# Gate and up columns taken 512 at a time instead of 256 in the dense layer and the experts

## The chip, the cores and the metric

One core of one Trainium2 chip. The metric is the device time of one execution in microseconds. The kernel before took 1407.61 us (median of 3 runs, 1405.66 to 1407.75).

## The reference, cut to what matters

Two layers on 256 tokens of width 1024. Each layer mixes the tokens (four mixers of 256 columns each) and then runs a feed-forward part: the first a dense SwiGLU, the second eight experts with two experts per token. D_FF is 2816. All in float32.

```
def swiglu(t, w_gate, w_up, w_down):
    return (jax.nn.silu(t @ w_gate) * (t @ w_up)) @ w_down
u = rms_norm(h, norm2_g[l])
f = swiglu(u, ffn_w_gate[j], ffn_w_up[j], ffn_w_down[j])          # layer 0
f = moe_ffn(u, moe_router[j], moe_w_gate[j], moe_w_up[j], moe_w_down[j])   # layer 1: swiglu of each routed token
h = h + f
```

## The kernel before, in words

**Weights stream through a ring.** All large weights are cut into pieces of 128 partitions x 2048 floats (1 MB). SyncE (SP) loads them in order into a ring of 11 slots, two DMAs a piece (L366). For each piece ScalarE (ACT) writes a rounded copy `high` (`split_high`, L531) and VectorE (DVE) the rest, `low` = piece - high (`split_low`, L861). Both have 3 slots, so the high of piece n waits until TensorE (PE) has used piece n-3 (`piece_used`). SP may load piece n when the low of piece n-11 is done. Every product is three matmuls: high x high, high x low, low x high (L1528 to L1530, L1504 to L1506).

**The feed-forward function `ffn`** stands once on each of ACT (L582), DVE (L900) and PE (L1488). It is called for the dense layer with two tiles of 128 tokens and for each expert job with one tile. It walks over 11 chunks of 256 gate and 256 up columns. The pieces of chunk c are a and b (four and four of the eight 128-row blocks, each row block with 256 gate and 256 up columns side by side, so one matmul of 512 columns gives both, in bank[t]) and d (256 rows of the down matrix). The order is a(0) b(0) a(1) b(1) d(0) a(2) b(2) d(1) ... b(10) d(9) d(10): 33 pieces (L61). With one tile a piece is 12 matmuls of 512 columns.

For chunk c the engines do:

- PE: the products of a and b; the down product of chunk c-1; then, when DVE's `hid` is there, two transposes for each tile into bank 4 (L1541). Chunk 10 is followed by its own down product (L1543).
- ACT: silu of the gate half (`sg`, L600), then the highs of the next pieces, then the rounded copy of the transposed block (`hTh`, L607).
- DVE: up x silu (`hid`, L916, L918 in the dense layer), lows, then `hTl` = bank 4 - hTh (L925).

**An expert job** works on the tokens of one expert; eight jobs run here, and none of the three spare ones. The work between jobs hangs on fixed chunks of the running job j: the result of job j-1 is rounded (`result_high` L825, `result_low` L1371) after the high and low of piece 1, and scattered by PE in chunk 0 (L1834); DVE adds it to h (`add_result`, L1379) in chunks 0 and 1; `slots` (L838, L1844) runs in chunk 2; DVE's selection of the next tokens in chunk 4 (L1394); PE gathers them in chunk 6 (L1816), ACT and DVE copy them out (`tokens_out`, L813, L1359), and PE transposes them in chunk 8 (L1825). At the last chunk ACT and DVE split these tokens (`tokens_high` L818, `tokens_low` L1364). In the first job DVE also plans the spare jobs in chunk 1 (`route_overflow`, L1320).

Of the kernel before, what the change touches and what calls it, by code (L numbers as in the profile page):

```python
# [56 lines left out]
CHUNKS = 11  # L57
N_FFN = 3 * CHUNKS
# [12 lines left out]

FFN_ORDER = ffn_pieces()
FFN_AT = {key: n for n, key in enumerate(FFN_ORDER)}

# [17 lines left out]
def build(nc, x, positions, norm1_g, w_in, mlstm_conv_w, mlstm_conv_b, mlstm_gate_b,  # L92
# [14 lines left out]
    F_CH = moe_w_gate.shape[3] // CHUNKS  # L107
    assert (TT, KD, F_CH, E) == (2, 8, 256, 8)
# [10 lines left out]
    with ctx:  # L119
# [102 lines left out]
        with ExitStack() as part:  # L222
            sg = sb("sg", [P, TT, 256], F32, part)
            hid = sb("hid", [P, TT, 256], F32, part)
            hTh = sb("hTh", [P, 2, TT, P], F32R, part)
            hTl = sb("hTl", [P, 2, TT, P], F32R, part)
# [74 lines left out]
        SLOTS_AT, SELECT_AT, GATHER_AT = 2, 4, 6  # L301
# [63 lines left out]
        def _(sp):  # L365
# [33 lines left out]
            def load_ffn(n0, wg, wu, wd, rounds=None):  # L399
                for i, (kind, c) in enumerate(FFN_ORDER):  # L400
                    n = n0 + i
                    if kind == "d":
                        dst = slot(n).rearrange("p (f n) -> p f n", f=2)
                        src = wd.rearrange("(f p) n -> p f n", p=P)
                        load(n, [(dst[:, f:f + 1, :], src[:, 2 * c + f:2 * c + f + 1, :]) for f in (0, 1)], rounds)
                    else:
# [3 lines left out]
                                  w.rearrange("(k p) n -> p k n", p=P)[:, k0:k0 + 4, c * F_CH:(c + 1) * F_CH])  # L410
# [117 lines left out]
        def _(act):  # L528
# [53 lines left out]
            def ffn(n0, job, job_n, tiles, after_split={}, after_chunk={}, after_last=None, scale=None, start=0):  # L582

# [10 lines left out]
                for c in range(CHUNKS):  # L594
                    at = FFN_AT[("b", c)]
# [22 lines left out]
            for l in range(DEPTH):  # L618
# [165 lines left out]
                if l == 0:  # L784
# [6 lines left out]
                    ffn(DENSE0, None, 0, TT, scale=rstd, start=2)  # L791
# [40 lines left out]
            def job(j, first):  # L832
# [8 lines left out]
                def next_tokens():  # L841

                    act.wait_ge(s["piece_used"], N_FFN * j + (MOE0 + FFN_AT[("b", CHUNKS - 1)] + 1))
# [14 lines left out]
        def _(dve):  # L858
# [41 lines left out]
            def ffn(n0, job, job_n, tiles, after_split={}, after_chunk={}, after_last=None, scale=None, start=0):  # L900
# [8 lines left out]
                for c in range(CHUNKS):  # L909
                    at = FFN_AT[("b", c)]  # L910
# [3 lines left out]
                    for t in range(tiles):  # L914
                        if scale is None:
                            last = dve.tensor_tensor(hid[:, t, :], bank[t][:, 256:512], sg[:, t, :], ALU.mult)  # L916
                        else:
                            last = dve.scalar_tensor_tensor(out=hid[:, t, :], in0=bank[t][:, 256:512], scalar=scale[:, t, 0:1],  # L918
                                                            in1=sg[:, t, :], op0=ALU.mult, op1=ALU.mult)
# [4 lines left out]
                    dve.wait_ge(s["hTh_ready"], job_n * CHUNKS + (c + 1))  # L924
                    dve.tensor_tensor(hTl[:, :, 0:tiles, :],  # L925
                                      bank[4][:, 0:2 * tiles * P].rearrange("p (f t n) -> p f t n", f=2, t=tiles),
                                      hTh[:, :, 0:tiles, :].bitcast(F32), ALU.subtract).then_inc(s["hTl_ready"], 1)
# [45 lines left out]
            for l in range(DEPTH):  # L973
# [271 lines left out]
                if l == 0:  # L1245
# [3 lines left out]
                    ffn(DENSE0, None, 0, TT, scale=rstd, start=2)  # L1249
# [129 lines left out]
            def add_result(n, t):  # L1379

                for half in range(2):
                    i = 2 * t + half
                    dve.wait_ge(s["scat_ready"], 4 * n - (3 - i))
                    dst = h[:, t, half * 512:(half + 1) * 512]
                    last = dve.tensor_tensor(dst, bank[SCATTER_BANKS[i]][:, :], dst, ALU.add).then_inc(s["added"], 1)

            def job(j, first):
# [16 lines left out]
                def chunk1():  # L1404
                    if first:
                        route_overflow()
                    else:
                        add_result(j, 1)
# [11 lines left out]
            for t in range(TT):  # L1420
                add_result(n_jobs, t)
# [12 lines left out]
        def _(pe):  # L1434
# [53 lines left out]
            def ffn(n0, job, job_n, tiles, xT, accs, first_claims, after_products={}):  # L1488


# [3 lines left out]
                def down(c):  # L1494
                    n = n0 + FFN_AT[("d", c)]
                    pe.wait_ge(s["hTl_ready"], at(c + 1))
                    pe.wait_ge(s["low_ready"], pieces + (n + 1))
                    for f in range(2):
# [391 lines left out]
```

## Time and profile before

| | |
|---|---|
| median of 3 runs | 1407.61 us |
| the profiled execution: device time / span | 1403.45 / 1401.7 us |
| PE busy | 1308.3 us (93%) |
| DVE busy | 1040.5 us (74%) |
| ACT busy | 825.3 us (59%) |
| read from HBM | 345.68 MB |
| dense `ffn` (first product to last) | 185.95 to 378.6 us |
| expert jobs (first product to last) | 570.97 to 1386.3 us |

The times of the table and of the rows come from one profiled execution. PE, DVE and ACT run beside each other, so their busy times don't add up. A matmul of 512 columns stands in the trace with some 390 ns, but the next one starts about 0.23 us after it: matmuls overlap, and the start-to-start distance is what counts.

### The profile page before, as it was taken

The numbers are of one execution on the slowest core, as the hardware profiler recorded it, in microseconds if no ns is written. First come the engines' busy times: TensorE is split into PE (matmuls) and PEld (weight loads), VectorE is DVE, ScalarE is ACT, GpSimd is POOL, SyncE is SP. The second block draws the span as 40 slices with busy tenths as digits, with TensorE's granted clock in tenths as the row PEclk, the third lists the DMA queues.
The fourth block names the chain that finished last, engine by engine and source line by source line (L and its number), as shares of the span: only waits on it lengthen the run. The fifth ranks groups of instructions, "written<-read, shape, count | busy, mean of one in ns | idle before, by whom it ended". The sixth has DMA issues, their size and how long they took to land.

```text
span 1401.7 us, 18029 instructions
## 1 busy us (share of the span) xinstructions
PE 1308.3 (93%) x6301; PEld 1081.8 (77%) x6301; DVE 1040.5 (74%) x1117; ACT 825.3 (59%) x886; POOL 33.3 (2%) x77
## 2 busy tenths in 40 slices
PE   4989979999899897899999999999999999999996
PEld 4967868888699586678788788787787887887884
DVE  4873645445469465588888988888988988988985
ACT  5333643344434264457776777777777677776774
POOL 4001000000000000000000000000000000000000
PEclk9986899999989868799999999999999999999998
DMA  9920345556354014489999999999999999999961
GB/s 303 321 79 2 113 155 189 181 183 176 115 188 151 1 60 136 148 294 345 333 352 350 321 362 346 325 365 342 317 354 331 350 347 333 342 353 338 344 225 46
DMA packets 267217, 347.43 MB, mean 248 GB/s; under 512 B 13166, under 2 KB 238592, under 8 KB 267168
## 3 DMA queue, kind: packets, MB, share of 16 engines
q1 hardware_dynamic: 265904, 344.43, 72.8%
q0 software_dynamic: 1232, 2.33, 0.7%
q8 instruction: 31, 0.51, 0.1%
q14 instruction: 18, 0.15, 0.0%
q10 hardware_dynamic: 32, 0.01, 0.0%
HBM read 345.68 MB, written 1.05 MB: 247 GB/s over the span
## 4 chain that ended last, share of the span: by engine, by line
PE 84%; DVE 11%; ACT 3%; issue 1%; DMA 1%; SPq 0%; DVEq 0%; ACTq 0%
PE bank L1528 15%; PE bank L1530 14%; PE bank L1529 14%; PE bank L1504 7%; PE bank L1505 7%; PE bank L1506 7%; DVE low L865 4%; DVE cacc L1005 3%; ACT high L538 2%; PE bank L1541 2%; PE bank L1816 1%; PE bank L1477 1%; PE bank L1478 1%; PE bank L1479 1%; PE bank L1772 1%
## 5 line engine op out<-in xcount | busy, mean ns | idle before, releaser
L865 DVE TENSOR_TENSOR low<-ring,high 128x2048 fp32r<-128x2048 f32 x327 | 743.0, 2283 | 166.7 <-ACT high L538 165.9
L538 ACT ACTIVATE high<-ring 128x2048 fp32r<-128x2048 f32 x327 | 623.1, 1908 | 168.6 <-PE bank L1530 99.6
L1528 PE MATMUL bank<-high,uTh 128*128 128x512 f32 x880 | 354.5, 403 | 11.8 <-DVE low L865 5.2
L1530 PE MATMUL bank<-high,uTl 128*128 128x512 f32 x880 | 346.1, 393 | 0.0
L1529 PE MATMUL bank<-low,uTh 128*128 128x512 f32 x880 | 344.7, 392 | 0.0
L1528 PEld LDWEIGHTS bank<-high,uTh 128*128 128x128 f32 x880 | 166.6, 189 | 46.8 <-DVE low L865 8.2
L1530 PEld LDWEIGHTS bank<-high,uTl 128*128 128x128 f32 x880 | 166.4, 189 | 36.3
L1529 PEld LDWEIGHTS bank<-low,uTh 128*128 128x128 f32 x880 | 166.9, 190 | 32.3
L1504 PE MATMUL bank<-high,hTh 128*128 128x512 f32 x440 | 176.8, 402 | 12.7 <-DVE hTl L925 9.4
L1505 PE MATMUL bank<-low,hTh 128*128 128x512 f32 x440 | 174.7, 397 | 0.0
L1506 PE MATMUL bank<-high,hTl 128*128 128x512 f32 x440 | 174.4, 396 | 0.0
L607 ACT ACTIVATE hTh<-bank 128x256 fp32r<-128x256 f32 (+1 forms) x99 | 40.2, 407 | 141.9 <-PE bank L1541 141.9
L1504 PEld LDWEIGHTS bank<-high,hTh 128*128 128x128 f32 x440 | 83.2, 189 | 35.6 <-issue 12.4
L1506 PEld LDWEIGHTS bank<-high,hTl 128*128 128x128 f32 x440 | 83.6, 190 | 19.9
L1505 PEld LDWEIGHTS bank<-low,hTh 128*128 128x128 f32 x440 | 83.6, 190 | 18.6
L600 ACT ACTIVATE sg<-bank 128x256 f32<-128x256 f32 x88 | 33.9, 386 | 70.4 <-PE bank L1530 70.4
L925 DVE TENSOR_TENSOR hTl<-bank,hTh 128x256 fp32r<-128x256 f32 (+1 forms) x99 | 44.5, 449 | 31.7 <-ACT hTh L607 31.7
L1477 PE MATMUL bank<-high,uTh 128*128 128x256 f32 (+2 forms) x192 | 54.1, 282 | 0.0
L1478 PE MATMUL bank<-low,uTh 128*128 128x256 f32 (+2 forms) x192 | 53.8, 280 | 0.0
L1479 PE MATMUL bank<-high,uTl 128*128 128x256 f32 (+2 forms) x192 | 53.7, 280 | 0.0
L1477 PE MATMUL bank<-uTh,high 128*128 128x256 f32 x160 | 47.3, 296 | 6.1 <-DVE uTl L895 6.1
L1005 DVE SCALAR_TENSOR_TENSOR cacc<-glu,cols,cacc 128x256 f32<-128x256 f32 x120 | 52.6, 508 | 0.0
(373 smaller groups left out, 1319.2 us busy)
## 6 DMA issues: line engine op xcount, KB each, us to landing
ring<-in_moe_w_gate_dram SPq DMA_DIRECT2D x176, 512.0 KB, 4.9
ring<-in_moe_w_up_dram SPq DMA_DIRECT2D x176, 512.0 KB, 6.1
ring<-in_moe_w_down_dram SPq DMA_DIRECT2D x176, 512.0 KB, 5.5
ring<-in_w_in_dram SPq DMA_DIRECT2D x36, 512.0 KB, 5.9
ring<-in_ffn_w_gate_dram SPq DMA_DIRECT2D x22, 512.0 KB, 4.0
ring<-in_ffn_w_up_dram SPq DMA_DIRECT2D x22, 512.0 KB, 5.0
ring<-in_ffn_w_down_dram SPq DMA_DIRECT2D x22, 512.0 KB, 3.8
ring<-in_w_out_dram SPq DMA_DIRECT2D x16, 512.0 KB, 6.2
```

What stands on the lines that cost most here:

```text
L538: act.activation(high[:, n % SPLIT, 0:width], slot(n)[:, 0:width], ACT.Copy).then_inc(s["high_ready"], 1)
L865: dve.tensor_tensor(low[:, n % SPLIT, 0:width], slot(n)[:, 0:width], high[:, n % SPLIT, 0:width].bitcast(F32), ALU.subtract).then_inc(s["l ...
L1005: ins = dve.scalar_tensor_tensor(out=cacc[:, c, :], in0=taps, scalar=w, in1=cacc[:, c, :], op0=ALU.mult, op1=ALU.add)
L1477: pe.matmul(dst, ah, bh, start=first, stop=False)
L1478: pe.matmul(dst, ah, bl, start=False, stop=False)
L1479: last = pe.matmul(dst, al, bh, start=False, stop=final)
L1504: pe.matmul(o, ah, bh, start=(c == 0 and f == 0), stop=False)
L1505: pe.matmul(o, ah, bl, start=False, stop=False)
L1506: last = pe.matmul(o, al, bh, start=False, stop=(c == CHUNKS - 1 and f == 1))
L1528: pe.matmul(o, ah, bh, start=(kd == 0), stop=False)
L1529: pe.matmul(o, ah, bl, start=False, stop=False)
L1530: last = pe.matmul(o, al, bh, start=False, stop=(kd == KD - 1))
```

## The change

Five chunks of 512 gate and 512 up columns and one of 256, in place of eleven of 256. A wide chunk has pieces u0, u1 (up, row blocks 0 to 3 and 4 to 7), g0, g1 (gate) and two down pieces d0, d1; the last chunk has a, b and d0 as before. The order is u0 u1 g0 g1 (0), then for c = 1 to 4 u0 u1 g0 g1 (c) d0 d1 (c-1), then a b (5) d0 d1 (4) d0 (5): still 33 pieces of 1 MB and two DMAs each. A gate or up row of a wide chunk is 2 KB in memory; it was 1 KB. Up goes to bank 0 (bank 1 for the second tile), gate to bank 4 (7 for the second), and the transposes of hid go over the gate bank. ACT, DVE and PE take a wide chunk with one instruction of 512 columns where there were two chunks with one of 256 each.

The order of the pieces and the chunks at which the work between jobs hangs:

```diff
 def ffn_pieces():
     for c in range(CHUNKS):
-        order += [("a", c), ("b", c)]
+        order += [("u0", c), ("u1", c), ("g0", c), ("g1", c)] if c < LAST else [("a", c), ("b", c)]
         if c:
-            order.append(("d", c - 1))
-    return order + [("d", CHUNKS - 1)]
+            order += [("d0", c - 1), ("d1", c - 1)]
+    return order + [("d0", LAST)]
...
-        SLOTS_AT, SELECT_AT, GATHER_AT = 2, 4, 6
+        UP_BANKS, GATE_BANKS = (0, 1), (4, 7)
+        DENSE_ACC, MOE_ACC = ((2, 3), (5, 6)), ((2, 3),)
+        SLOTS_AT, GATHER_AT = 2, 3
```

`ffn` on ACT (`product_end(c)` is the index of g1, or of b in the last chunk; `blocks(c)` is 4, in the last chunk 2):

```diff
                 for c in range(CHUNKS):
-                    at = FFN_AT[("b", c)]
+                    at = product_end(c)
+                    w = 128 * blocks(c)
                     upto(at + 2)
...
-                        last = act.activation(sg[:, t, :], bank[t][:, 0:256], ACT.Silu,
+                        gate = bank[GATE_BANKS[t] if c < LAST else UP_BANKS[t]]
+                        last = act.activation(sg[:, t, 0:w], gate[:, 0:w], ACT.Silu,
                                               scale=1.0 if scale is None else scale[:, t, 0:1])
                     last.then_inc(s["silu_ready"], 1)
-                    if c == CHUNKS - 1 and after_last:
+                    upto(at + (3 if c in (0, LAST) else 4))
+                    if c == LAST and after_last:
                         after_last()
-                    upto(at + 3)
                     act.wait_ge(s["hid_tr"], job_n * CHUNKS + (c + 1))
-                    act.activation(hTh[:, :, 0:tiles, :],
-                                   bank[4][:, 0:2 * tiles * P].rearrange("p (f t n) -> p f t n", f=2, t=tiles),
-                                   ACT.Copy).then_inc(s["hTh_ready"], 1)
+                    for t in range(tiles):
+                        last = act.activation(hTh[:, 0:blocks(c), t, :],
+                                              bank[GATE_BANKS[t]][:, 0:w].rearrange("p (f n) -> p f n", n=P), ACT.Copy)
+                    last.then_inc(s["hTh_ready"], 1)
...
-                ffn(MOE0, j, j + 1, 1, {} if first else {1: lambda: result_high(j)},
+                ffn(MOE0, j, j + 1, 1, MOE_TILES, {} if first else {2: lambda: result_high(j)},
```

`ffn` on DVE and what a job hangs into it:

```diff
                     last.then_inc(s["hid_ready"], 1)
-                    if c == CHUNKS - 1 and after_last:
+                    after_hid.get(c, lambda: None)()
+                    upto(at + (3 if c in (0, LAST) else 4))
+                    dve.wait_ge(s["hTh_ready"], job_n * CHUNKS + (c + 1))
...
+                    last.then_inc(s["hTl_ready"], 1)
+                    if c == LAST and after_last:
                         after_last()
-                    upto(at + 3)
...
-                ffn(MOE0, j, j + 1, 1, {} if first else {1: lambda: result_low(j)},
-                    {0: chunk0, 1: chunk1, SELECT_AT: next_select, GATHER_AT: lambda: tokens_out(j + 1)},
+                        add_result(j, 2)
+
+                ffn(MOE0, j, j + 1, 1, MOE_TILES, {} if first else {2: lambda: result_low(j)},
+                    {} if first else {1: lambda: add_result(j, 1), 2: lambda: add_result(j, 3)},
+                    {0: chunk0, 1: chunk1, SLOTS_AT: next_select, GATHER_AT: lambda: tokens_out(j + 1)},
```

`ffn` on PE (a product piece is 12 matmuls for each tile, as before, into one bank):

```diff
+                def hidden_transposes(c):
+                    pe.wait_ge(s["hid_ready"], at(c + 1))
+                    for t in range(tiles):
+                        for f in range(blocks(c)):
+                            last = pe.transpose(bank[GATE_BANKS[t]][:, f * P:(f + 1) * P], hid[:, t, f * P:(f + 1) * P], ident[:, :])
+                    last.then_inc(s["hid_tr"], 1)
...
                 for c in range(CHUNKS):
+                    if c < LAST:
+                        products("u0", c)
+                        products("u1", c)
+                        if c:
+
+                            pe.wait_ge(s["hTl_ready"], at(c))
+                        products("g0", c)
+                        products("g1", c)
+                    else:
+                        products("a", c)
+                        products("b", c)
                     if c:
...
+                        down(c - 1, 0)
+                        if c < LAST:
+                            down(c - 1, 1)
                     after_products.get(c, lambda: None)()
...
+                    hidden_transposes(c)
+                down(LAST - 1, 1)
+                down(LAST, 0)
...
-                        GATHER_AT + 2: lambda: gathered_transposes(j + 1)}
+                        GATHER_AT + 1: lambda: gathered_transposes(j + 1)}
```

In the expert jobs `add_result` now adds one quarter at a time: quarters 0 and 2 after hTl of chunks 0 and 1, quarters 1 and 3 after hid of chunks 1 and 2. `route_overflow` stays in chunk 1.

## Rows read from the trace of the kernel before

**Rows 1.** The page, part 4: the chain that ended last, by engine.
```profile
PE 84%; DVE 11%; ACT 3%; issue 1%; DMA 1%; SPq 0%; DVEq 0%; ACTq 0%
```

**Rows 2.** Windows, one expert job: length, engines' busy us (instructions), PEclk, DMA share, GB/s.
```profile
840.40:941.40 101.00, 99.21 (x450) 80.69 (x449) 88.42 (x69) 72.27 (x62) 0.00 (x0) 1.00 1.00 343
```

**Rows 3.** Waits of PE and of SP's DMA queue in the same job: us, times, longest.
```profile
PE bank L1504 <- DVE hTl L925: 1.0, 1, 1.0
PE bank L1528 <- DVE low L865: 0.8, 1, 0.8
...
SPq L375 <- DVE low L865: 62.9, 33, 5.1
```

**Rows 4.** Timeline of PE at a job's end: start us, us, instruction, idle before.
```profile
877.00 0.38 PE L1541 MATMUL bank<-ident,hid 128*128 128x128 f32 x2
878.39 0.49 PE L1504 MATMUL bank<-high,hTh 128*128 128x512 f32 x1 [1.01 <-DVE hTl L925]
...
881.04 0.39 PE L1506 MATMUL bank<-high,hTl 128*128 128x512 f32 x1
882.21 0.50 PE L1528 MATMUL bank<-high,uTh 128*128 128x512 f32 x1 [0.78 <-DVE low L865]
```

**Rows 5.** Timeline of PE where nothing is waited for: transposes, two pieces, down.
```profile
951.69 0.38 PE L1541 MATMUL bank<-ident,hid 128*128 128x128 f32 x2
951.83 0.47 PE L1528 MATMUL bank<-high,uTh 128*128 128x512 f32 x1
952.14 0.39 PE L1529 MATMUL bank<-low,uTh 128*128 128x512 f32 x1
...
957.40 0.40 PE L1504 MATMUL bank<-high,hTh 128*128 128x512 f32 x1
```

**Rows 6.** Timeline of ACT at a job's end and the next one's start.
```profile
877.42 0.38 ACT L607 ACTIVATE hTh<-bank 128x256 fp32r<-128x256 f32 x1 [1.66 <-PE bank L1541]
877.91 3.72 ACT L538 ACTIVATE high<-ring 128x2048 fp32r<-128x2048 f32 x2
881.54 1.25 ACT L829 ACTIVATE yh<-bank,wslot 128x512 fp32r<-128x512 f32 x2
```

**Rows 7.** Timeline of DVE at the same place.
```profile
876.17 1.28 DVE L1367 TENSOR_TENSOR uTl<-bank,uTh 128x512 fp32r<-128x512 f32 x2
...
879.86 4.49 DVE L865 TENSOR_TENSOR low<-ring,high 128x2048 fp32r<-128x2048 f32 x2 [1.60 <-ACT high L538]
884.27 1.40 DVE L1375 SCALAR_TENSOR_TENSOR yl<-bank,wslot,yh 128x512 fp32r<-128x512 f32 x2
```

**Rows 8.** Groups by line and shape: count, busy us, mean ns, idle before.
```profile
L916 DVE TENSOR_TENSOR hid<-bank,sg 128x256 f32<-128x256 f32 x88 | 36.8, 418 | 13.0 <-ACT sg L600 13.0
...
L925 DVE TENSOR_TENSOR hTl<-bank,hTh 128x512 fp32r<-128x512 f32 x11 | 7.6, 691 | 20.0 <-ACT hTh L607 20.0
L607 ACT ACTIVATE hTh<-bank 128x512 fp32r<-128x512 f32 x11 | 6.6, 597 | 35.5 <-PE bank L1541 35.5
```

**Rows 9.** Dense layer: PE's waits in the layer, then ACT and DVE in chunk 0.
```profile
PE bank L1541 <- DVE hid L918: 1.8, 1, 1.8
PE bank L1504 <- DVE hTl L925: 1.4, 1, 1.4
...
199.62 0.84 ACT L600 ACTIVATE sg<-bank,rstd 128x256 f32<-128x256 f32 x2 [3.46 <-PE bank L1530]
200.49 0.88 DVE L918 SCALAR_TENSOR_TENSOR hid<-bank,rstd,sg 128x256 f32<-128x256 f32 x2 [6.33 <-ACT sg L600]
```

**Rows 10.** First job's long wait (timeline of PE); windows after it and at the kernel's end.
```profile
598.14 0.76 PE L1504 MATMUL bank<-high,hTh 128*128 128x512 f32 x1 [3.33 <-DVE low L865]
...
598.10:603.40 5.30, 5.26 (x12) 4.02 (x13) 4.63 (x3) 0.00 (x0) 0.00 (x0) 0.50 0.78 252
...
1386.30:1389.30 3.00, 0.15 (x1) 0.00 (x0) 1.41 (x2) 2.55 (x3) 0.00 (x0) 1.00 0.02 5
1389.30:1393.00 3.70, 3.51 (x8) 2.26 (x8) 1.65 (x4) 0.72 (x1) 0.00 (x0) 0.54 0.00 0
```

More of the change, by code:

```diff
@@ L222, in build @@
         with ExitStack() as part:
[L223 to L226, printed above, removed]
+            sg = sb("sg", [P, TT, WIDE], F32, part)
+            hid = sb("hid", [P, TT, WIDE], F32, part)
+            hTh = sb("hTh", [P, 4, TT, P], F32R, part)
+            hTl = sb("hTl", [P, 4, TT, P], F32R, part)
+        with ExitStack() as part:
+            moe_sg = sb("moe_sg", [P, 1, WIDE], F32, part)
+            moe_hid = sb("moe_hid", [P, 1, WIDE], F32, part)
+            moe_hTh = sb("moe_hTh", [P, 4, 1, P], F32R, part)
+            moe_hTl = sb("moe_hTl", [P, 4, 1, P], F32R, part)
             unh = sb("unh", [P, TT, D], F32R, part)
@@ L298, in build @@
         SCATTER_BANKS = (1, 5, 6, 7)
-        SLOTS_AT, SELECT_AT, GATHER_AT = 2, 4, 6
+        UP_BANKS, GATE_BANKS = (0, 1), (4, 7)
+        DENSE_ACC, MOE_ACC = ((2, 3), (5, 6)), ((2, 3),)
+        DENSE_TILES, MOE_TILES = (sg, hid, hTh, hTl), (moe_sg, moe_hid, moe_hTh, moe_hTl)
+        SLOTS_AT, GATHER_AT = 2, 3
         fin_g = ring[:, 0, 0:D]
@@ L580, in group_rstd, with ffn @@
                 act.activation(rstd[:, :, g:g + 1], lnv[:, :, g:g + 1], ACT.Exp, scale=-0.5).then_inc(s["group_rstd"], 1)
-            def ffn(n0, job, job_n, tiles, after_split={}, after_chunk={}, after_last=None, scale=None, start=0):
+            def ffn(n0, job, job_n, tiles, sets, after_split={}, after_chunk={}, after_last=None, scale=None, start=0):
+                sg, _, hTh, _ = sets
                 done = [start]
@@ L898, in gains_of, with ffn @@
                 last.then_inc(s["utl_ready"], 1)
-            def ffn(n0, job, job_n, tiles, after_split={}, after_chunk={}, after_last=None, scale=None, start=0):
+            def ffn(n0, job, job_n, tiles, sets, after_split={}, after_hid={}, after_chunk={}, after_last=None, scale=None, start=0):
+                sg, hid, hTh, hTl = sets
                 done = [start]
@@ L1377, in result_low, with add_result @@
                 last.then_inc(s["yl_ready"], 1)
[L1379 to L1385, printed above, removed]
+            def add_result(n, i):
+                t, half = divmod(i, 2)
+                dve.wait_ge(s["scat_ready"], 4 * n - (3 - i))
+                dst = h[:, t, half * 512:(half + 1) * 512]
+                dve.tensor_tensor(dst, bank[SCATTER_BANKS[i]][:, :], dst, ALU.add).then_inc(s["added"], 1)
             def job(j, first):
@@ L1486, in uT, with ffn, products, down @@
                 return uTh[:, k, lo:hi], uTl[:, k, lo:hi]
-            def ffn(n0, job, job_n, tiles, xT, accs, first_claims, after_products={}):
+            def ffn(n0, job, job_n, tiles, sets, xT, accs, first_claims, after_products={}):
+                _, hid, hTh, hTl = sets
                 pieces = N_FFN * job if job is not None else 0
                 at = lambda c: job_n * CHUNKS + c
-                def down(c):
-                    n = n0 + FFN_AT[("d", c)]
+                def products(kind, c):
+                    n = n0 + FFN_AT[(kind, c)]
+                    kh = {"u0": 0, "g0": 0, "a": 0, "u1": 1, "g1": 1, "b": 1}[kind]
+                    pe.wait_ge(s["low_ready"], pieces + (n + 1))
+                    if job is None and c == 0 and kind[0] == "u":
+                        pe.wait_ge(s["utl_ready"], 4 * 2 + 2 * (kh + 1))
+                    for t in range(tiles):
+                        o = bank[GATE_BANKS[t] if kind[0] == "g" else UP_BANKS[t]][:, :]
+                        for k in range(4):
+                            kd = 4 * kh + k
+                            ah, al = xT(kd, t)
+                            bh, bl = part(n, k * 512, (k + 1) * 512)
+                            pe.matmul(o, ah, bh, start=(kd == 0), stop=False)
+                            pe.matmul(o, ah, bl, start=False, stop=False)
+                            last = pe.matmul(o, al, bh, start=False, stop=(kd == KD - 1))
+                    last.then_inc(s["piece_used"], 1)
+                def down(c, half_of):
+                    n = n0 + FFN_AT[(f"d{half_of}", c)]
                     pe.wait_ge(s["hTl_ready"], at(c + 1))
                     pe.wait_ge(s["low_ready"], pieces + (n + 1))
-                    for f in range(2):
+                    for i in range(2):
+                        f = 2 * half_of + i
                         for t in range(tiles):
@@ L1502, in down @@
                                 ah, al = hTh[:, f, t, :], hTl[:, f, t, :]
[L1503 removed]
+                                bh, bl = part(n, i * 1024 + half * 512, i * 1024 + half * 512 + 512)
                                 pe.matmul(o, ah, bh, start=(c == 0 and f == 0), stop=False)
                                 pe.matmul(o, ah, bl, start=False, stop=False)
[L1506 removed]
+                                last = pe.matmul(o, al, bh, start=False, stop=(c == LAST and f == 1))
```

92 lines of the change are left out of this document (38 added, 54 removed).

## Prediction, made before the change was run

> **What bounds the kernel now.** I read the chain of waits first: PE holds 84% of it, DVE 11% [rows 1]. The longest stage is the eight expert jobs, so I looked at one job by windows: 101.0 us, of which PE is busy 99.2, DVE 88.4 and ACT 72.3, with the granted clock at 1.00, the upper of its two levels (2.4 GHz) [rows 2]. The waits of that job say what PE lacks: it waits only twice, once at its end for hTl (1.0 us) and once at the next job's first product for a low (0.8 us) [rows 3]. Everything else is matmuls end to end. The arithmetic of a job is the same after the change (88 products and 44 down products, each of three matmuls of 512 columns, and 22 transposes), so its floor is the same too. What can change is these two waits, new waits of the same kind, and the clock.
>
> **Durations.** Two product pieces (24 matmuls) take 5.57 us (951.83 to 957.40), a piece 2.8 us; two transposes take 0.14 us to the next product, whose first step is 0.31 instead of 0.23 us [rows 5]. Four transposes I put at 0.36. PE waiting costs, beyond the wait, about 0.1 us of slower first step (the same row; after transposes it is paid anyway).
>
> **Part 1: the last chunk's wait goes.** Before, the transposes of chunk 10 start at 877.00 and the down product that needs them at 878.39, 1.39 us, against 0.14 where nothing is waited for [rows 4, 5]; nothing is left for PE to do meanwhile. After, d1(4), 2.8 us, stands between the transposes of the last chunk and d0(5). Is hTl there in time? Count from the start of d0(4). ACT: silu 0.2 to 0.6; high of the last piece (two take 3.72 [rows 6], so 1.9) to 2.4; tokens_high, as long as DVE's 1.28 pair at most [rows 7], to 3.6; hTh to 4.0. DVE: low of the last piece (2.2 to 2.3 [rows 7]) to 4.7, hTl 0.4, to 5.1. PE wants it at 2.8 + 0.14 + 2.8 = 5.7. So 1.25 us a job are saved, 8 x 1.25 = **-10.0 us**.
>
> **Part 2: the wait at a job's start nearly goes.** Before, the last down matmul starts at 881.04 and the next job's first at 882.21: 1.17 where 0.23 is normal, 0.94 lost and 0.1 of restart [rows 4]; the high of piece 0 begins behind hTh at 877.91 and the low at 879.86 [rows 6, 7]. Seven times: -7.2. After, going on with the count: DVE does tokens_low behind hTl, 5.1 + 1.3 = 6.4, then the low of the next job's piece 0 to 8.6 or 8.7, and ACT's high of it is done by 5.9. PE is at the next job at 2.8 + 0.14 + 2.8 + 2.8 = 8.55. I take 0.1 us of wait and 0.1 of restart, +1.4 in seven jobs. Net **-5.8 us**. Pieces 1 to 3 follow at a low every 2.2 us against 2.8 on PE; result_low (1.40 [rows 7]) stands ahead of piece 3's low, which ends some 7.9 us after the job's start, and PE wants it at 8.2.
>
> **Part 3: a new chain, in each wide chunk.** g0(c+1) overwrites the gate bank with the transposes in it, and its high is made behind hTh. PE covers this with u0 and u1, 5.57 us. The chain, from the start of u0: hTh starts at 0.28 (877.42 is 0.42 after 877.00 [rows 4, 6], less the 0.14 to the next product), takes 0.60 [rows 8], high 1.9, low 2.3, and 0.1 to PE: 5.2. It holds by 0.4 us where nothing is hung in between. In chunk 2, selT and wslot stand between hTh and high; I put them at 0.4, so it is even. In chunk 3, tokens_out, a copy as wide as hTh (0.60 [rows 8]), makes it 5.8: 0.2 of wait and 0.1 of restart, 8 x 0.3 = **+2.4 us**. Bounds: nothing (if the copies overlap by 0.1 each, as the pairs do: 1.25 for two), or 0.5 in both chunks, +8. hTl itself (0.69 [rows 8]) is ready about 1.6 after u0 starts if DVE is free, at the worst behind a low and an addition, 3.5, still in time.
>
> **Part 4: instructions saved.** Two of 256 columns become one of 512: hid 2 x 0.418 to 0.69, and so hTl (0.69), sg and hTh (0.60 against 2 x 0.38) [rows 8, 6]. DVE gains about 1.5 us a job and ACT as much. Neither ends a wait by its sum, so in the total this is 0; it helps DVE, which is at 88 of 101 us, to keep parts 2 and 3 in time.
>
> **Part 5: the dense layer.** Its last-chunk wait of 1.4 us [rows 9] goes under d1(4), twice as long here (two tiles): **-1.5 us** with the restart. In chunk 0 nothing covers silu and hid: before, PE waits 1.8 us for a pair of each, 0.84 and 0.88 [rows 9]. 512 wide, a pair with a scale takes 1.25 on ACT and 1.40 on DVE [rows 6, 7]: 0.41 + 0.52 = **+0.9 us**, and the wait becomes 2.8.
>
> **Part 6: the clock after that wait.** In this trace a wait of 1.8 us left the clock at its upper level. After 3.33 us of idle PE it stood at 0.50, 1.2 GHz, and 12 matmuls took 5.3 us where 2.8 is normal; after the 2.9 us of idle at the kernel's end it stood at 0.54 [rows 10]. 2.8 is nearest to that last one, so I take a fall of the clock once, **+2.5 us**; the bounds are 0 and 3. The waits of up to 1.4 us elsewhere don't come near.
>
> **Part 7: the first expert job.** In chunk 0 there is no scatter to cover silu and hid: 0.60 and 0.69 in place of 0.38 and 0.42, **+0.5 us** [rows 6, 8]. In the other jobs the scatter, eight matmuls or 1.8 us, covers the 1.6 they need. Its 3.3 us wait behind route_overflow [rows 10] stays: those small instructions again stand between an hTl and the low that PE wants next as before, and u0, u1 cover as much as a, b did. 0, bounds -1 and +1.
>
> **Part 8: transfers.** In a job SP's queue waits 62.9 of 101 us for a free slot [rows 3], and no high waits for a transfer, so faster transfers give 0. The same 34.6 MB in 99.2 us need 349 GB/s in place of 343 [rows 2].
> The Trainium skill, "DMA: Bandwidth & Descriptors", section "Why small descriptors are slow (HBM only)", charges each packet three fixed cycles beside one for each 32 bytes. By an estimate from that page 2 KB rows spend 4.5% on them and 1 KB rows 8.6%, so that a stage bound by transfers would gain some 3%, and one bound by PE nothing. No row here shows 2 KB rows.
>
> **Sum.** -10.0 - 5.8 + 2.4 - 1.5 + 0.9 + 2.5 + 0.5 = -11.0 us. The profiled execution took 1403.45 us, so it would take 1392.5; the median of the runs is 4.2 us higher than the profiled one, and against it the forecast is 1407.6 - 11.0 = **1396.6 us**. 0.2% of it, 2.8 us, is about what a measurement can tell from no change.
>
> **Rivals.**
> (A) All chains of parts 2, 3 and 6 end in time: no +1.4, +2.4, +2.5; -17.3, 1390.3 us. For it speak the overlaps of about 0.1 us between neighbours on one engine, against it the idle row at the end. Chance 0.10.
> (B) The waits removed come back in part: parts 2 and 3 at their upper bounds, a start wait of 0.5 us (+2.8 more) and +8 in place of +2.4: 1405 would be the worst, the middle 1401. DVE's order (low, hTl, tokens_low, low) has no slack at the job's start, which speaks for it. Chance 0.12.
> (C) Slower: in every wide chunk the chain of part 3 is late. Four places a job are followed by a g0, 32 in all. The forecast's -11 is used up at 0.34 us a place with the restart, that is if the chain lasts 0.64 us longer than my 5.2. If DVE is 1 us behind there, because lows, additions and hTl queue up (88 of 101 us busy), PE waits 0.6 + 0.1: 32 x 0.7 = 22, less the 2.4 counted: 1416 us. Against it: the chunks without extras leave DVE idle before each low, as they do now. Chance 0.07.
> (D) The clock doesn't hold. PE now writes its products by turns to two banks and the down products to two more. If it fell once a job at the price of rows 10, 2.5 us, the time would be 1396.6 + 20 = 1417 us. The granted clock of 1.00 through a job that already changes banks every 12 or 24 matmuls and waits 1 us twice [rows 2, 3] speaks against it. Chance 0.03.
> The Trainium skill, "TensorE: Matmul & The Clock Gate", section "A second HAM failure mode: psum-queue depth-cycling", reports for another kernel that cycling through banks idles PE so often that its clock goes up and down; by that rule (D) would come. The trace of before doesn't agree, at 1.00.
> (E) The change doesn't do what it says for the experts, because 343 GB/s is all the transfers give: DMA share 1.00 [rows 2]. Then a job stays at 101 us and only the dense layer and the clock count, -1.5 + 0.9 + 2.5 + 0.5 = +2.4: 1410 us. SP's queue waiting 62.9 us for slots speaks against it. Chance 0.05.
>
> **Chances and range.** The forecast has 0.63. Faster by over 0.2% are the forecast, (A) and most of (B): 0.84; within 0.2%: a rest of (B) and a part of (E), 0.05; slower: (C), (D), most of (E): 0.11. The range from 1390 to 1403 us holds the forecast with its bounds, (A) and most of (B), and leaves out some 0.18.
>
> **What the changed profile would show.** A job of 99.1 us by windows; no wait of L1504's successor for hTl in the last chunk; the first product of a job 0 to 0.3 us after its time; at most 0.3 us before g0 in chunk 4; in the dense layer one wait of 2.8 us before the first transposes, and the clock after it at 0.5. Wrong would be: a wait before g0 in chunks 1 and 2 (then part 3's chain is mis-sized, C), a job that still takes 101 us with highs waiting for a DMA (E), or a granted clock under 1.00 within the jobs (D).

## The result and the profile after

Median of four runs after: 1387.82 us (1382.03 to 1390.85); of four before: 1406.63 us (1403.36 to 1407.75). The ratio is 0.9865, with a 95% interval of 0.9828 to 0.9902. So the change saves 18.8 us where 11.0 were forecast. The sign was right; the time lies 2.2 us under the range, and the forecast's own gain is outside the interval. The profiled execution took 1387.18 us, its span is 1385.3 us, against 1403.45 and 1401.7.

First the page of after, parts 1, 2 and 4 (busy us and share of the span, DMA packets, the chain that ended last). The last answers to [rows 1]:

```profile
PE 1308.3 (94%) x6301; PEld 1089.4 (79%) x6301; DVE 1032.4 (75%) x1028; ACT 817.7 (59%) x797; POOL 32.9 (2%) x77
...
DMA packets 175057, 347.43 MB, mean 251 GB/s; under 512 B 13166, under 2 KB 54272, under 8 KB 175008
...
PE 87%; DVE 10%; ACT 1%; issue 1%; DMA 1%; SPq 0%; DVEq 0%; ACTq 0%
```

PE's share of the chain rose from 84 to 87%, DVE's fell from 11 to 10. Packets fell from 267,217 to 175,057. Where the time went stands in the windows. Here those of before, from the first product to the last down product of the dense layer, of the mixers between, and of the eight expert jobs (length, busy us and instructions of PE, PEld, DVE, ACT, POOL, granted clock, DMA share, GB/s):

```profile
185.95:378.58 192.63, 189.38 (x836) 154.80 (x836) 89.81 (x65) 81.68 (x74) 0.00 (x0) 0.99 0.54 172
378.60:571.00 192.40, 163.92 (x970) 143.35 (x969) 127.61 (x251) 83.69 (x158) 9.64 (x13) 0.80 0.31 105
570.97:1386.30 815.33, 797.82 (x3576) 648.25 (x3576) 701.14 (x561) 571.33 (x491) 0.00 (x0) 0.99 0.95 322
```

And after, with one steady job, which answers to [rows 2]:

```profile
187.56:379.25 191.69, 188.89 (x836) 154.96 (x836) 87.59 (x56) 80.26 (x65) 0.00 (x0) 0.99 0.54 173
379.30:576.50 197.20, 170.79 (x969) 149.41 (x969) 127.71 (x251) 83.81 (x158) 9.67 (x13) 0.78 0.30 102
576.53:1370.48 793.95, 789.35 (x3576) 647.24 (x3576) 694.77 (x481) 564.92 (x411) 0.00 (x0) 1.00 0.93 331
...
843.65:942.15 98.50, 98.50 (x450) 80.91 (x449) 87.61 (x59) 71.48 (x52) 0.00 (x0) 1.00 0.98 352
```

By the starts of their first and last matmuls the dense layer went from 192.4 to 191.5 us (-0.9), the experts from 815.1 to 793.7 (-21.4). The mixers between them went from 192.6 to 197.5 (+4.9) although nothing in them was changed: the same 970 matmuls were busy for 170.8 in place of 163.9 us at a granted clock of 0.78 in place of 0.80. The start of the kernel is 1.6 us longer and the tail 0.5 shorter. Together -16.3 us, the difference of the two profiled executions; that of the medians is 2.5 more (one of the four runs on either side was profiled). The two changed stages alone differ by -22.3.

In the steady job PE is busy for all of 98.50 us, and no matmul of it waits. The queue of SP still waits for slots, for 61.6 of 98.5 us, as in [rows 3]:

```profile
SPq L397 <- DVE low L895: 61.6, 33, 4.8
```

At the job's end, PE and then DVE (start, us, instruction, idle before), for [rows 4, 7]:

```profile
872.14 0.38 PE L1570 MATMUL bank<-ident,moe_hid 128*128 128x128 f32 x2
872.28 0.48 PE L1561 MATMUL bank<-high,moe_hTh 128*128 128x512 f32 x1
...
877.71 0.40 PE L1563 MATMUL bank<-high,moe_hTl 128*128 128x512 f32 x1
877.95 0.39 PE L1544 MATMUL bank<-high,uTh 128*128 128x512 f32 x1
```

```profile
873.97 0.42 DVE L958 TENSOR_TENSOR moe_hTl<-bank,moe_hTh 128x256 fp32r<-128x256 f32 x1
874.31 1.28 DVE L1403 TENSOR_TENSOR uTl<-bank,uTh 128x512 fp32r<-128x512 f32 x2
875.50 6.89 DVE L895 TENSOR_TENSOR low<-ring,high 128x2048 fp32r<-128x2048 f32 x3
```

Both waits are gone. The last down matmul starts at 877.71 and the next job's first product at 877.95, 0.24 us, the normal step; before it was 1.17 [rows 4]. The low that it needs starts at 875.50 and takes 2.3 of the 6.89 us, so it ends at 877.8, just ahead.

The dense layer's first chunk and the first job's long wait (PE), for [rows 9, 10]:

```profile
214.87 1.09 PE L1570 MATMUL bank<-ident,hid 128*128 128x128 f32 x8 [2.80 <-DVE hid L951]
...
617.87 0.47 PE L1544 MATMUL bank<-high,uTh 128*128 128x512 f32 x1 [3.18 <-DVE low L895]
```

```profile
214.80:220.00 5.20, 5.13 (x27) 4.41 (x28) 5.20 (x5) 1.46 (x3) 0.00 (x0) 1.00 0.34 91
617.80:623.00 5.20, 5.13 (x23) 4.30 (x24) 4.44 (x3) 1.92 (x1) 0.00 (x0) 1.00 0.77 260
```

The dense wait is 2.80 us, as worked out, but the clock behind it stands at 1.00. It also stands at 1.00 behind the 3.18 us of the first job, where it fell to 0.50 before [rows 10].

In what follows a gap is the time from one matmul's start to the next one's; where it should be 0.23 us, what is above that is the wait. It holds a little more than the idle time in brackets, since a matmul's end reaches past its successor's start.

### The profile page after: what moved, and what is told of

It reads as the page before. It is cut to its first block, busy times and chain, and to the rows that moved or that the text cites. A ratio compares the mean times of both kernels' runs of the same rounds, so it can differ in the third digit from the quotient of the medians.

```text
span 1385.3 us, 17674 instructions
## 1 busy us (share of the span) xinstructions
PE 1308.3 (94%) x6301; PEld 1089.4 (79%) x6301; DVE 1032.4 (75%) x1028; ACT 817.7 (59%) x797; POOL 32.9 (2%) x77
## 2 busy tenths in 40 slices
DMA packets 175057, 347.43 MB, mean 251 GB/s; under 512 B 13166, under 2 KB 54272, under 8 KB 175008
## 4 chain that ended last, share of the span: by engine, by line
PE 87%; DVE 10%; ACT 1%; issue 1%; DMA 1%; SPq 0%; DVEq 0%; ACTq 0%
PE bank L1544 15%; PE bank L1546 14%; PE bank L1545 14%; PE bank L1561 7%; PE bank L1562 7%; PE bank L1563 7%; DVE cacc L1041 3%; DVE low L895 2%; PE bank L1570 2%; PE bank L1867 1%; PE bank L1514 1%; PE bank L1515 1%; PE bank L1516 1%; PE bank L1823 1%; PE bank L1824 1%; PE bank L1825 1%
## 5 line engine op out<-in xcount | busy, mean ns | idle before, releaser
L1544 PE MATMUL bank<-high,uTh 128*128 128x512 f32 x880 | 350.0, 398 | 9.9 <-DVE uTl L925 4.0
L1561 PE MATMUL bank<-high,moe_hTh 128*128 128x512 f32 x352 | 139.9, 397 | 0.0
L1562 PE MATMUL bank<-low,moe_hTh 128*128 128x512 f32 x352 | 138.9, 395 | 0.0
L1563 PE MATMUL bank<-high,moe_hTl 128*128 128x512 f32 x352 | 138.9, 394 | 0.0
L1563 PEld LDWEIGHTS bank<-high,moe_hTl 128*128 128x128 f32 x352 | 66.3, 188 | 15.7
L1562 PEld LDWEIGHTS bank<-low,moe_hTh 128*128 128x128 f32 x352 | 66.5, 189 | 15.1
L1561 PEld LDWEIGHTS bank<-high,moe_hTh 128*128 128x128 f32 x352 | 66.3, 188 | 14.9
L637 ACT ACTIVATE moe_hTh<-bank 128x512 fp32r<-128x512 f32 (+1 forms) x48 | 27.1, 564 | 68.3 <-PE bank L1570 68.3
L629 ACT ACTIVATE moe_sg<-bank 128x512 f32<-128x512 f32 (+1 forms) x48 | 27.1, 564 | 38.5 <-PE bank L1546 38.5
L1515 PE MATMUL bank<-uTl,high 128*128 128x256 f32 x160 | 47.2, 295 | 0.0
```

Of the source, the lines that this page charges most:

```text
L1515: pe.matmul(dst, ah, bl, start=False, stop=False)
L1544: pe.matmul(o, ah, bh, start=(kd == 0), stop=False)
L1561: pe.matmul(o, ah, bh, start=(c == 0 and f == 0), stop=False)
L1562: pe.matmul(o, ah, bl, start=False, stop=False)
L1563: last = pe.matmul(o, al, bh, start=False, stop=(c == LAST and f == 1))
```

## The experiments

Each ratio is against runs of the kernel before on the same chip: 1409.08 us in experiments 1 to 4 (14 runs), 1408.04 in 5 to 8 (11 runs), 1411.98 in 9 (3 runs).

**1. The tail order alone, on the kernel before.** The last chunk of a job has its second down half behind the transposes and its hidden blocks in the unused second tile slot:

```diff
                     if c:
-                        down(c - 1)
+                        down(c - 1, (0,) if tail else (0, 1))
...
                     last.then_inc(s["hid_tr"], 1)
+                    if tail:
+                        down(c - 1, (1,))
```

> The kernel before, still with chunks of 256 and 1 KB rows, but in the last chunk of an expert job the transposes stand in the middle of d(9), so that six matmuls (1.4 us) lie between them and the last down product. Theory 1 (the gain of the expert jobs is the two waits at a job's end and start, and the order there removes both; width and rows give nothing): a job falls from 101.0 to 98.7 to 99.2 us, the whole by 14 to 18 us. Theory 2 (wider instructions and 2 KB rows give it): a job stays at 100.7 to 101.0 us. In between, about 99.8: only the end wait goes and the start wait stays.

1402.48 us, ratio 0.9955 (0.994 to 0.997); a job takes 100.38 us. PE at the job's end:

```profile
878.81 0.44 PE L1546 MATMUL bank<-ident,hid 128*128 128x128 f32 x2 [0.55 <-DVE hid L917]
879.00 0.48 PE L1507 MATMUL bank<-high,hTh 128*128 128x512 f32 x1
...
884.08 0.50 PE L1532 MATMUL bank<-high,uTh 128*128 128x512 f32 x1 [0.60 <-DVE low L866]
```

None of the three expectations held: the order alone gives 0.6 of the 2.5 us a job. The wait for hTl is gone, but a wait of 0.55 us for hid stands in front of the transposes, and of the 0.78 at the next job's start 0.60 stay. In the kernel before one down piece, 12 matmuls or 2.8 us, stands between the last two chunks, and cut in two it leaves 1.4 us on either side of the transposes. That is enough for hTh and hTl, but silu and hid take 0.7 us longer than that (the gap there is 0.94 in place of 0.23), and the next job's first high still begins behind hTh. With wide chunks the narrow last one follows a chunk with two down pieces, so that a whole piece, 2.8 us, stands on either side, and a piece more, 5.6 us in place of 4.2, between the transposes and the next job, for the low that starts it. So what counts is the order together with the wide chunk ahead of it.

One thing beside the point turns up here: behind the dense layer's first wait, 1.84 us of idle as in the kernel before and with the same code up to there, the clock fell.

```profile
202.00:206.00 4.00, 4.00 (x14) 3.25 (x13) 4.00 (x3) 0.98 (x2) 0.00 (x0) 0.61 0.24 48
```

**2. The tail order undone, on the kernel after.** Both down pieces of chunk 4 stand again ahead of the last transposes:

```diff
-                        if c < LAST:
-                            down(c - 1, 1)
+                        down(c - 1, 1)
...
-                down(LAST - 1, 1)
                 down(LAST, 0)
```

> The changed kernel with both down pieces of chunk 4 ahead of the last transposes, so that nothing stands between these and the last down product. Theory 1: the end wait of about 1.25 us comes back in every job, and the start wait in part, as the high of the next job's first piece is again behind a late hTh: a job of 99.8 to 100.9 us in place of 98.5. Theory 2: a job stays at 98.5 to 98.7 us.

1402.4 us over ten runs, 1390.31 to 1410.66, ratio 0.9952 (0.9915 to 0.999). The scatter is wide, the profile is plain: a steady job takes 100.77 us. PE at its end:

```profile
875.43 0.49 PE L1561 MATMUL bank<-high,moe_hTh 128*128 128x512 f32 x1 [1.01 <-DVE moe_hTl L958]
...
879.24 0.50 PE L1544 MATMUL bank<-high,uTh 128*128 128x512 f32 x1 [0.78 <-DVE low L895]
```

These are the two waits of before to the hundredth, 1.01 and 0.78 us [rows 4]. 2.3 of the 2.5 us a job hang on this order of PE in the last chunk, given the wide chunk ahead of it (experiment 1); parts 1 and 2 are shown. The kernel after also has another order on ACT (the last high ahead of tokens_high) and on DVE (hTl ahead of tokens_low) there. It stands in this run too, so by itself it ends neither wait; whether the gain needs it, no run tests. The mixers took 191.8 us here at a clock of 0.81 with the code of after, so their 197.5 us isn't forced by the change.

**3. The rows alone undone, on the kernel after.** The same 2048 columns of a piece in two transfers of 256 columns of every row:

```diff
-load(n, [(dst[:, k:k + 2, :], src[:, k0 + k:k0 + k + 2, c * WIDE:(c + 1) * WIDE]) for k in (0, 2)], rounds)
+load(n, [(dst[:, :, g:g + 256], src[:, k0:k0 + 4, c * WIDE + g:c * WIDE + g + 256]) for g in (0, 256)], rounds)
```

> The changed kernel with 1 KB rows: each wide piece is loaded in two DMAs of 256 columns. Theory 1 (PE bounds the jobs, transfers have slack): a job stays at 98.5 us and the whole within 0.2%. Theory 2 (2 KB rows are needed for 98.5 us): a job of 99.5 to 101 us, with highs waiting for a DMA.

1389.83 us, ratio 0.9863 (0.9843 to 0.9882), that of after being 0.9865. The steady jobs start 98.47 to 98.51 us apart, in after 98.50 to 98.53. One of them by windows, and SP's queue in it:

```profile
837.30:935.80 98.50, 98.50 (x450) 80.92 (x449) 87.64 (x59) 71.48 (x52) 0.00 (x0) 1.00 1.03 349
...
SPq L397 <- DVE low L895: 59.0, 33, 4.4
```

The queue waits 59.0 us for slots in place of 61.6, and 267,217 packets carry what 175,057 did. What the rows do change is the transfer engines' busy share: 1.03 at 349 GB/s with 1 KB, 0.98 at 352 with 2 KB in the job above, some 5% less time for a byte. In the time of the kernel the 2 KB rows are worth nothing here.

**4. One more copy in the chain ahead of g0.** Behind hTh in chunks 0 to 3 of each job, on the kernel after:

```diff
                     last.then_inc(s["hTh_ready"], 1)
+                    if job is not None and c < LAST - 1:
+                        act.activation(sg[:, 0, :], sg[:, 0, :], ACT.Copy)
```

> The changed kernel with one more ACT copy of 512 columns (about 0.5 us) between hTh and the next high, in chunks 0 to 3 of each job; it measures the slack of the chain hTh, high, low, g0. If neighbours on an engine overlap by 0.1 us (chain 5.0 us plain, 5.3 in chunk 2, 5.5 in chunk 3, against 5.57 of cover): waits of 0.2 to 0.3 us in chunk 2 and 0.4 to 0.5 in chunk 3, none in chunks 0 and 1, a job of 99.0 to 99.5 us. If the prediction's sum of full durations were right (5.2, 5.6, 5.8): waits in chunks 1, 2 and 3 of 0.2, 0.6 and 0.8, a job of about 100.3 us.

1396.58 us, ratio 0.9916 (0.9894 to 0.9938). A job took 99.70 us, +1.2, 0.2 above what was expected for the shorter chain and 0.6 under that for the longer. 0.9 of it are two gaps: 0.59 us behind chunk 2 (0.36 of wait) and 0.76 behind chunk 3 (0.53). Some 0.1 of slower restart each comes with chunks 1 and 2, where the gap behind chunk 1 is 0.26; chunk 0 took the copy without a trace. The last product ahead of chunk 3's gap and the one behind it, then ACT there:

```profile
853.81 0.39 PE L1548 MATMUL bank<-high,uTl 128*128 128x512 f32 x1
854.57 0.50 PE L1546 MATMUL bank<-high,uTh 128*128 128x512 f32 x1 [0.37 <-DVE low L897]
```

```profile
848.78 0.60 ACT L637 ACTIVATE moe_hTh<-bank 128x512 fp32r<-128x512 f32 x1 [3.14 <-PE bank L1572]
849.27 0.62 ACT L641 ACTIVATE moe_sg<-moe_sg 128x512 f32<-128x512 f32 x1
849.79 0.59 ACT L848 ACTIVATE u<-bank 128x512 f32<-128x512 f32 x1
850.27 1.92 ACT L566 ACTIVATE high<-ring 128x2048 fp32r<-128x2048 f32 x1
```

Starts are 0.49, 0.52 and 0.48 us apart where the rows say 0.60, 0.62 and 0.59: neighbours on an engine overlap by about 0.1 us. So the copy costs 0.52 in the chain, and all of it (0.53) shows as a wait in chunk 3. In other words chunk 3 had hardly any slack and no wait, chunk 2 had 0.16 and chunk 1 about 0.5. The same place in the kernel after, PE, ACT and DVE:

```profile
944.34 0.48 PE L1544 MATMUL bank<-high,uTh 128*128 128x512 f32 x1
...
949.89 0.50 PE L1544 MATMUL bank<-high,uTh 128*128 128x512 f32 x1
...
944.62 0.60 ACT L637 ACTIVATE moe_hTh<-bank 128x512 fp32r<-128x512 f32 x1 [3.15 <-PE bank L1570]
945.11 0.59 ACT L846 ACTIVATE u<-bank 128x512 f32<-128x512 f32 x1
945.59 3.72 ACT L566 ACTIVATE high<-ring 128x2048 fp32r<-128x2048 f32 x2
...
947.54 4.49 DVE L895 TENSOR_TENSOR low<-ring,high 128x2048 fp32r<-128x2048 f32 x2 [1.00 <-ACT high L566]
```

From 944.34 to the end of the first low at 949.83 (a pair of them takes 4.49, one 2.29) are 5.49 us, and u0 and u1 last 5.55.

**5. One more operation behind tokens_low, on DVE, in the last chunk:**

```diff
                     if c == LAST and after_last:
                         after_last()
+                        dve.tensor_tensor(hid[:, 0, :], sg[:, 0, :], sg[:, 0, :], ALU.mult)
```

> The changed kernel with one more DVE operation of 512 columns (about 0.5 to 0.6 us) behind tokens_low; it measures the slack of the chain at a job's start (hTl, tokens_low, low of piece 0, first product). The trace of the changed kernel shows 0.1 us of slack there: a wait of 0.3 to 0.5 us at seven job starts with 0.1 of restart, a job of 98.9 to 99.1 us. By the prediction's part 2, which had no slack, 0.1 more. If the start hung on ACT's high instead, a job stays at 98.5 us.

1390.97 us, ratio 0.9882 (0.9847 to 0.9917); a job took 99.07 us. DVE and PE at the job's start:

```profile
877.75 0.68 DVE L964 TENSOR_TENSOR moe_hid<-moe_sg 128x512 f32<-128x512 f32 x1
878.35 4.49 DVE L895 TENSOR_TENSOR low<-ring,high 128x2048 fp32r<-128x2048 f32 x2
...
880.69 0.50 PE L1545 MATMUL bank<-high,uTh 128*128 128x512 f32 x1 [0.33 <-DVE low L895]
```

The extra operation moves the low by 0.60 us and the gap is 0.73, a wait of 0.50. So the slack at the job's start was 0.1 us, where part 2 had put a wait of 0.1.

**6. The overflow work of the first job spread out.** What route_overflow did at once behind chunk 1 is done behind chunks 0, 1, 2 and 4, on the kernel after:

```diff
-                    if first:
-                        route_overflow()
+                    if first:
+                        overflow_job(0)
...
+                def chunk2():
+                    next_select()
+                    if first:
+                        overflow_job(1)
+
+                def chunk4():
+                    overflow_job(2)
+                    overflow_end()
```

> The changed kernel with route_overflow in parts, one for each spare job, behind hTl of chunks 0, 1, 2 and 4 of the first job. The wait of 3.3 us before g0 of chunk 2 goes, and no fall of the clock can follow it: the experts' stage falls from 793.7 to about 790.3 us, the periods of the other jobs stay at 98.5 us. Against the kernel before a ratio of 0.984. Rival: the wait is only cut into pieces before several g0, 1 us or more of it left.

1381.35 us, ratio 0.9816 (0.9786 to 0.9847). The experts take 790.4 us, 3.3 less than after. PE's waits in the first 65 us of the expert stage, in full:

```profile
PE bank L1561 <- DVE uTl L1409: 2.7, 1, 2.7
PE bank L1587 <- DVE moe_hid L949: 1.4, 1, 1.4
```

The 3.18 us wait is gone, nothing takes its place.

**7. The gate products ahead of the up products in chunk 0,** so that silu is made under the up products, on the kernel after:

```diff
+        if c == 0:
+            order += [("g0", c), ("g1", c), ("u0", c), ("u1", c)]
...
-                    act.wait_ge(s["piece_used"], (N_FFN * job if job is not None else 0) + (n0 + at + 1))
+                    act.wait_ge(s["piece_used"], (N_FFN * job if job is not None else 0) + (n0 + (at + 1 if c else 2)))
...
+                    if c == 0:
+                        dve.wait_ge(s["piece_used"], (N_FFN * job if job is not None else 0) + (n0 + at + 1))
```

> The changed kernel with gate ahead of up in chunk 0, so that silu runs under the up products and only hid is left behind them. Dense layer: the wait before the first transposes falls from 2.96 to about 1.65 us; first job: from 1.57 to about 0.95 us; the later jobs, where the scatter covers it, stay at 98.5 us. Sum -1.9 us. Rival: the highs of pieces 4 and 5, which now come behind silu, are late and a wait of the same size stands before u0 or u1 of chunk 1.

1385.81 us, ratio 0.9848 (0.982 to 0.9876). The first transposes of the dense layer, the first job's long wait and a window behind it:

```profile
209.49 1.09 PE L1575 MATMUL bank<-ident,hid 128*128 128x128 f32 x8 [1.57 <-DVE hid L956]
...
607.05 0.47 PE L1549 MATMUL bank<-high,uTh 128*128 128x512 f32 x1 [3.18 <-DVE low L898]
...
607.00:612.30 5.30, 5.25 (x16) 4.22 (x17) 4.30 (x2) 0.77 (x1) 0.00 (x0) 0.68 0.76 267
```

The dense layer took 190.0 us, 1.5 less (its gap went from 3.19 to 1.96), and the first job's gap before its transposes from 1.80 to 1.24. The experts as a whole stayed at 793.8, because here the clock fell for 3.4 us after the first job's long wait, which is the same in code and length as in after. That costs more than the 0.56 of the gap; against it the clock stood at its lower level for 3.7 us at the start of the stage and not 5.4.

**8. Both, 6 and 7 together.**

> Both edits of the two runs before in the changed kernel: -5.2 us against it if they add up, about 1382.5 us and a ratio to the kernel before of 0.983; the experts' stage 789.7 us and the dense layer 190.2 us. If the mixers' clock differs as between the profiles so far (their stage took 191.8 to 197.5 us), the single profile can hide it; the two stages can't.

1382.49 us, ratio 0.9808 (0.9776 to 0.984). Its windows for the dense layer and the experts:

```profile
185.90:376.30 190.40, 188.83 (x836) 155.03 (x836) 87.67 (x56) 80.34 (x65) 0.00 (x0) 0.99 0.52 174
...
575.30:1365.50 790.20, 789.29 (x3576) 647.08 (x3576) 695.46 (x481) 565.82 (x411) 0.00 (x0) 1.00 0.93 333
```

The dense layer is 1.2 us under after and the experts 3.7. In the totals experiments 6 and 8 can't be told apart: the runs of either spread by 6 to 12 us, and the mixers took 199.1 us in the profile of 8 and 197.6 in that of 6. Both are faster than the kernel before; that they are faster than the change alone is shown by the stages, while the intervals of the totals overlap with its.

**9. A longer wait in the dense layer's first chunk.** Two more copies on ACT between silu and hid, on the kernel after, to see whether the clock falls at all there:

```diff
                                               scale=1.0 if scale is None else scale[:, t, 0:1])
+                    if job is None and c == 0:
+                        for extra in range(2):
+                            last = act.activation(scratch[:, extra, :], bank[GATE_BANKS[0]][:, :], ACT.Copy)
```

> The changed kernel with two more ACT copies of 512 columns behind silu in chunk 0 of the dense layer: PE's wait before the first transposes grows from 2.96 to about 4.0 us; nothing else changes. If part 6 of the prediction had its size right and only the length of the wait wrong, the clock falls to 0.5 after it and the dense layer takes 191.5 + 1.0 + 2.5 = 195.0 us. If a wait of this length may or may not lower the clock, depending on when it comes, it can also be 192.5 us; one run tells only whether it falls here and what it then costs.

1387.16 us, ratio 0.9825 (0.9749 to 0.99), from two runs. Behind a gap of 4.17 us the clock did fall:

```profile
210.30:214.10 3.80, 0.09 (x1) 0.00 (x0) 1.40 (x3) 3.67 (x5) 0.00 (x0) 1.00 0.00 0
214.10:220.00 5.90, 5.84 (x23) 4.81 (x24) 5.61 (x5) 1.45 (x3) 0.00 (x0) 0.71 0.44 140
```

The layer took 194.0 us, 2.5 more than after: 1.0 of longer wait and 1.5 for 3.4 us at the lower of the two levels. That is between the 192.5 and the 195.0 expected; one profile shows that the clock can fall here, not how often.

## Why the forecast was too small

In the two stages that the change touches the profiles differ by -0.9 - 21.4 = -22.3 us; the forecast had -11.0. Point by point:

- **Part 1, right.** The end wait of 1.25 us a job is gone, and comes back to the hundredth when the order is undone (2). The count of when hTl would be there held: 5.1 us from the start of d0(4). In the trace d0(4) starts 2.8 us ahead of the transposes at 872.14, and hTl ends at 873.97 + 0.42, 5.05 us later.
- **Part 2, right in its mechanism, a term 0.2 us a job too careful.** I had 8.6 or 8.7 us for the low against PE at 8.55, and took 0.1 of wait and 0.1 of restart. In the trace the low is there after 8.45 us and PE after 8.6; experiment 5 puts the slack at 0.1. +1.4 us that were not to be paid.
- **Part 3, the step that failed by its own numbers.** I added 0.60 of hTh, 0.60 of the copy, 1.9 and 2.3 as the rows give them one by one. The time from start to start is 0.49, 0.48, 1.95 and 2.3, and the chain with the step to PE is at most 5.55, not 5.8 (4): 0.2 of the difference are the overlaps, the rest is the step to PE, which I had put at 0.1. [Rows 6] had shown it, two highs in 3.72 us, and I used the overlap as a bound only. In the steady job the chain decides nothing, though by as little as 0.06 us. Of the 8 x 0.3 only the slower restart in chunk 3, some 0.1 us a job, is there (949.89 to the next product at 950.23, 0.34 where 0.23 is normal). +2.4 us counted, at most +0.9 measured.
- **Part 4, right in its 0, its size half.** DVE and ACT did less (701.1 to 694.8 us, 571.3 to 564.9 in the expert stage), 0.8 us a job each where 1.5 were worked out. With the tail order undone (2), wide instructions and all else together leave 0.2 us a job.
- **Part 5, right.** -0.6 net forecast, -0.9 measured. The wait became 2.80 us.
- **Part 6, the second step that failed.** I took the fall of the clock from the nearest row, 2.9 us of idle at the kernel's end. At 2.8 us of idle in this place the clock stayed up in all six profiles that had that wait (after and experiments 2 to 6), while in experiment 1 it fell for 3.4 us behind the shorter wait of before, 2.23 us by the gap. +2.5 us that didn't come.
- **Part 7, its +0.5 right, its 0 for the long wait a failed step too.** The first transposes' gap went from 1.32 to 1.80. But behind the long wait, which stayed (3.18 us for 3.33), the clock had fallen in [rows 10], and I let it fall again by saying nothing. It didn't: 12 matmuls at 0.23 and not 0.43 us, some -2.5. It is not a gain of the change either but luck of these two profiles: with that wait at 3.2 to 3.3 us of idle the clock fell in before and experiments 1, 4, 7 and 9, and not in after and 2, 3 and 5.
- **Part 8, right (3).** SP's queue waited for slots 59.0 us a job with 1 KB rows and 61.6 with 2 KB, and 349 GB/s served as well as 352. The overhead of small packets in the Trainium skill, "DMA: Bandwidth & Descriptors", section "Why small descriptors are slow (HBM only)", shows here in the engines' busy share alone, some 5% less for a byte where the estimate from that page was 3%. No stage that loads these rows is bound by transfers, so no run shows what it would give in time.

-11.0 less 1.4, 2.4, 2.5 and 2.5 is -19.8. Of the 2.5 us left 0.3 are the dense layer's, and some 1.5 are 0.2 us in each of seven steady jobs, which shrank by 2.5 us where the two waits and a restart were 2.3. These 0.2 lie in no wait: with both waits back the job of experiment 2 is still 0.2 under that of before. The forecast put nothing for the seams between chunks. Transposes of before that are two chunks apart, and of after that are one wide chunk apart:

```profile
915.80 0.38 PE L1541 MATMUL bank<-ident,hid 128*128 128x128 f32 x2
...
932.83 0.38 PE L1541 MATMUL bank<-ident,hid 128*128 128x128 f32 x2
...
890.72 0.60 PE L1570 MATMUL bank<-ident,moe_hid 128*128 128x128 f32 x4
...
907.64 0.60 PE L1570 MATMUL bank<-ident,moe_hid 128*128 128x128 f32 x4
```

The same matmuls and transposes take 17.03 us as two chunks and 16.92 as one, 0.1 for this pair. Over the five pairs of a job, with 0.1 taken back by the slower restart in chunk 3, that comes near the 0.2. Another 0.3 us is no part of the change: at the start of the expert stage the clock stood at its lower level for 6.0 us before and 5.4 after. The rest I can't place.

The rivals: the kernel went the way of (A), all chains in time; the 1390.3 us worked out for it lacks the first job's clock and that 0.2. (B) and (C) turned on an engine queueing up behind; no chain was late. (D) is refuted for this kernel, since the clock is 1.00 through jobs whose products change banks every 24 matmuls. The Trainium skill, "TensorE: Matmul & The Clock Gate", section "A second HAM failure mode: psum-queue depth-cycling", reports the clock going up and down in a kernel whose PE is briefly idle between its groups of matmuls. This trace has the changes of bank without the idling, PE busy for 98.50 of 98.50 us, and no fall, so changing banks alone doesn't do it here. (E) is refuted: transfers ran at 352 GB/s when PE took more.

The range failed because its lower end was (A)'s time as it stood. Three of my terms, together 6.3 us, could each be 0 by my own account and were all entered at a cost; with all at 0 the time was 1390.3, and the range had nothing left below that for anything I hadn't counted, while the untouched mixers alone moved by several us from profile to profile. It should have reached below (A) for that.

## What to carry to other kernels

Sum a chain of small instructions by the time from start to start, not by their durations: here four links were 0.2 us too long by the latter, and the wait that was forecast was 0.2. When a wait on the engine that bounds the kernel is put under other work, ask how much work stands on each side of it: 1.4 us on either side only moved the wait (1), 2.8 us ended it (2). Price a fall of the clock as something that may or may not happen, on both sides of the comparison.

## What the runs showed of the chip that I had not expected

- Whether TensorE's clock falls behind a wait of some 2 to 4 us depends on more than its length. 2.8 us of idle in the dense layer: 0 of 6 fell. The 1.84 us of before: not in before, but in experiment 1, with the same code up to there. 3.2 to 3.3 us in the first job: fell in 5 of 9. When it falls, it costs 1.5 us (3.4 us at the lower level, experiment 9) to some 2.5 (6.8 us, before).
- The mixers' stage, the same code in all of them (kernel before and after alike), took between 191.8 and 199.1 us in eleven profiles, at a granted clock of 0.81 to 0.78. Some 7 us, against the 22.3 that the change saves in its two stages, lie in a stage that it doesn't touch, so stages tell more here than totals. With two profiles of the kernel before (192.6 and 194.6 us) it stays open whether the mixers are slower on average behind the change.
- Neighbours on ACT or DVE overlap by 0.1 us: 0.60 us long, 0.49 apart; two of 2048 columns take 3.72 and 4.49 us where one takes 1.92 and 2.29.
